# Four matrix products of a decoder layer: weight fetch, input split and norm moved into one stage each

## The chip, the cores and the metric

The kernel runs on one core of a Trainium2 chip. The metric is the device time of one execution in microseconds (us); the kernel before took 5367.47 us (median of 3 runs, 5363.57 to 5371.20).

## The reference, cut to what matters

One inference step of one decoder layer, for 1024 prompt tokens and 64 sample tokens (1088 together), width 1024:

```
h = h + [GatedDeltaNet | Mamba2-SSD](rmsnorm(h) @ w_in) @ w_out     # w_out is 2048 x 1024
h = h + attention(rmsnorm(h, g_xattn) @ w_xq, memory) @ w_xo        # both 1024 x 1024
f = rmsnorm(h, g_ffn)
h = h + peer(f, f @ w_pq)                                           # w_pq is 1024 x 2048
y = rmsnorm(h, g_final)

rmsnorm(x, w) = x * rsqrt(mean(x*x) + 1e-6) * w
```

The change touches the products with w_out, w_xq, w_xo and w_pq and the two norms ahead of w_xq and w_pq. The delta net, the state space scan (SSD), the attention, the top-16 retrieval and the experts are as they were.

## The kernel before, in words

Activations lie transposed: a [128, 8, 1088] tile has the width in 8 slices of 128 partitions (k = 0 to 7) and the tokens along the free dimension, in three chunks of 384, 384 and 320 columns. The residual `h` stays in SBUF from the first of the four products on.

Every product is done in split precision. A 32-bit operand x becomes hi = round(x) in the 32-bit type that TensorE multiplies in one pass, and lo = x - hi; `split_product` (lines 123 to 128) then issues three matmuls, hi*hi, lo*hi and hi*lo, into one PSUM bank. The hi half is an ACT copy; the lo half is a subtraction on DVE or POOL.

`linear` (from line 1557) makes a product. It goes through the outputs in blocks of 128, two to a turn of a hardware loop; r = 0, 1 says which. For a block: SP fetches 512 KB of weights (line 1584), ACT rounds them to `w_hi` (1610), POOL subtracts for `w_lo` (1623), TensorE does 3 chunks x 8 slices x 3 matmuls = 72 matmuls (1633), chunk outermost, slice k inside, and DVE adds the three banks to the residual (1654) or copies them to a stage that SP stores (1650, 1589). Each of these has two buffers, so the weights of a block are made ready while an earlier block is multiplied. The two r's use PSUM banks 0 to 2 and 3 to 5.

`split_tiles` (line 1665) is a stage of its own ahead of three of the products: SP loads (1674), ACT copies each slice to hi (1681), DVE takes the lo of the even slices (1687) and POOL that of the odd ones (1693). Ahead of the other two products stands `rmsnorm` (line 131): ACT squares the 8 slices (164), DVE adds them up (212), TensorE sums over the partitions with 9 matmuls against ones (181; the trace counts 18 instructions), DVE, ACT and DVE make 1/root (214, 167, 216), TensorE spreads it over the partitions (185), DVE multiplies (221, 24 instructions), and the result is split as above (172, 194). Every stage is a `Block` inside a `Phase`: it begins when all engines have ended the one before, and its own weight fetch can begin only then.

The order in `trunk` (from line 2616) is: SSD; `split_tiles` heads_dn; `linear` w_heads_dn (first half of w_out); `split_tiles` heads_ssm; `linear` w_heads_ssm; `rmsnorm` att_norm; `linear` w_xq; attention; `split_tiles` attended; `linear` w_xo; `rmsnorm` ffn_norm; `linear` w_pq; the rest. The SP queue is in program order: a transfer behind a waiting one is not issued.

## Time and profile before

| what | us |
|---|---|
| median of 3 runs | 5367.47 |
| the profiled execution, its own time | 5374.69 |
| its span, first to last instruction | 5372.9 |
| TensorE busy in the span | 4552.5 (85%) |
| w_heads_dn product, first matmul to last | 1762.1 to 1860 |
| w_heads_ssm | 1885.5 to 1983.2 |
| w_xq | 2034.6 to 2131 |
| w_xo | 2321.0 to 2417.8 |
| w_pq | 2469.5 to 2662 |

The times in the lower rows count from the first instruction of the span. Between the products lie the stages that split and normalize; between w_xq and w_xo also the attention, and ahead of w_heads_dn the end of the SSD.

### The profile page before, as it was taken

Reading aid. Unit: us, or ns where it says so; the run is one execution under the profiler, and the core shown is the slowest. Engines: PE = TensorE matmul, PEld = TensorE weight load, DVE = VectorE, ACT = ScalarE, POOL = GpSimd, SP = SyncE. Lnnn points to the kernel's source line nnn. Section 1 sums busy time; section 2 is a strip of 40 time slices with the busy share of each in tenths; the row PEclk is TensorE's granted clock in tenths of the full one; section 3 lists DMA queues with packets and bytes.
Section 4 is the critical chain, followed back from the end, with each engine's and each line's share of the span. In section 5 each row is a group of like instructions: output and inputs, shape, how many; then the busy total and the mean of one; then the engine's idle time right before and its main releaser. Section 6 shows DMA issues by size and latency. Waiting matters only on the chain. (4 is left out here: it accounts for less than half of the span.)

```text
span 5372.9 us, 72522 instructions
## 1 busy us (share of the span) xinstructions
PE 4552.5 (85%) x26809; PEld 4074.5 (76%) x26809; DVE 3182.0 (59%) x6516; ACT 1485.7 (28%) x2869; POOL 1715.0 (32%) x985
## 2 busy tenths in 40 slices
PE   6999999978785777776835666999999999999996
PEld 4677777765553777576834656999999999999996
DVE  2454455534555121212199995777787887778786
ACT  2233333312222111112003552333333333333332
POOL 0111111111111212022102444555555555555552
PEclk9999999989897888988967888999999999999998
DMA  4111111112212202402212437878888887787885
GB/s 149 50 38 44 48 42 37 38 38 59 67 50 84 96 29 85 154 32 99 76 33 79 124 93 252 294 284 291 291 300 291 289 291 282 285 295 288 284 301 189
DMA packets 339412, 825.70 MB, mean 154 GB/s; under 512 B 44334, under 2 KB 227038, under 8 KB 284766
## 3 DMA queue, kind: packets, MB, share of 16 engines
q1 hardware_dynamic: 247006, 373.65, 20.9%
q0 software_dynamic: 55296, 402.68, 20.7%
q10 hardware_dynamic: 36864, 46.15, 2.7%
q8 instruction: 147, 2.41, 0.2%
q14 instruction: 99, 0.81, 0.0%
HBM read 730.19 MB, written 92.21 MB: 153 GB/s over the span
## 5 line engine op out<-in xcount | busy, mean ns | idle before, releaser
L126 PE MATMUL psum_banks<-f_dense_hi,exp_u_hi 128*128 128x352 f32 x2048 | 665.4, 325 | 72.1 <-POOL exp_u_lo L2358 54.4
L2564 DVE CUSTOM_DVE_ANT_0 residual<-residual,f_rows 128x1024 f32<-128x1024 f32 x384 | 672.4, 1751 | 43.1 <-DMA residual<-in_peer_rows,pick_index 42.6
L2367 POOL DMA_INDIRECT residual<-in_peer_rows,pick_index x384 | 516.1, 1344 | 564.1 <-DVE psum_banks L2576 500.1
L126 PE MATMUL psum_banks<-exp_hidden_hi,exp_v_hi 128*128 128x352 f32 x2048 | 660.9, 323 | 8.6 <-issue 7.2
L127 PE MATMUL psum_banks<-f_dense_lo,exp_u_hi 128*128 128x352 f32 x2048 | 661.8, 323 | 0.0
L128 PE MATMUL psum_banks<-f_dense_hi,exp_u_lo 128*128 128x352 f32 x2048 | 661.7, 323 | 0.0
L127 PE MATMUL psum_banks<-exp_hidden_lo,exp_v_hi 128*128 128x352 f32 x2048 | 659.6, 322 | 0.0
L128 PE MATMUL psum_banks<-exp_hidden_hi,exp_v_lo 128*128 128x352 f32 x2048 | 659.4, 322 | 0.0
L663 PE MATMUL psum_banks<-x_normed,dn_weights 128*128 128x384 f32 (+1 forms) x1536 | 526.6, 486 | 20.7 <-DMA dn_conv_w<-in_dn_conv_w 20.7
L2576 DVE SCALAR_TENSOR_TENSOR psum_banks<-residual,exp_coefs,psum_banks 128x1024 f32<-128x1024 f32 x381 | 487.4, 1279 | 0.0
L126 PEld LDWEIGHTS psum_banks<-f_dense_hi,exp_u_hi 128*128 128x128 f32 x2048 | 387.2, 189 | 82.0 <-POOL exp_u_lo L2358 31.6
L953 POOL TENSOR_TENSOR dn_block<-dn_lower,dn_level_masks 128x1152 f32<-128x1152 f32 x56 | 147.2, 2635 | 835.4 <-DVE dn_lower L1027 787.9
L663 PEld LDWEIGHTS psum_banks<-x_normed,dn_weights 128*128 128x128 f32 x1536 | 286.6, 198 | 161.4 <-DMA dn_conv_w<-in_dn_conv_w 21.5
L126 PEld LDWEIGHTS psum_banks<-exp_hidden_hi,exp_v_hi 128*128 128x128 f32 x2048 | 385.3, 188 | 11.3 <-issue 7.4
L2358 POOL TENSOR_TENSOR exp_v_lo<-exp_stage,exp_v_hi 128x1024 fp32r<-128x1024 f32 x128 | 312.5, 2442 | 244.4 <-ACT exp_v_hi L2465 243.4
L128 PEld LDWEIGHTS psum_banks<-f_dense_hi,exp_u_lo 128*128 128x128 f32 x2048 | 387.2, 189 | 0.0
L127 PEld LDWEIGHTS psum_banks<-f_dense_lo,exp_u_hi 128*128 128x128 f32 x2048 | 387.2, 189 | 0.0
L127 PEld LDWEIGHTS psum_banks<-exp_hidden_lo,exp_v_hi 128*128 128x128 f32 x2048 | 385.4, 188 | 0.0
L128 PEld LDWEIGHTS psum_banks<-exp_hidden_hi,exp_v_lo 128*128 128x128 f32 x2048 | 385.4, 188 | 0.0
L2483 ACT ACTIVATE exp_dot_gelus<-exp_dots 128x1 f32<-128x1 f32 x384 | 77.9, 203 | 1020.6 <-DVE exp_dots L2564 1020.4
L2358 POOL TENSOR_TENSOR exp_u_lo<-exp_stage,exp_u_hi 128x1024 fp32r<-128x1024 f32 x128 | 314.1, 2460 | 94.0 <-ACT exp_u_hi L2465 92.8
L2130 POOL TENSOR_TENSOR route_onehots<-route_onehots,route_picked_gates_t 128x512 f32<-128x512 f32 x176 | 183.3, 1041 | 437.9 <-DVE route_onehots L2228 423.7
(465 smaller groups left out, 8643.3 us busy)
## 6 DMA issues: line engine op xcount, KB each, us to landing
exp_stage<-in_peer_u SPq DMA_DIRECT2D x128, 512.0 KB, 4.6
exp_stage<-in_peer_v SPq DMA_DIRECT2D x128, 512.0 KB, 4.0
exp_gates<-expert_gates ACTq DMA_DIRECT2D x256, 176.0 KB, 4.2
expert_gates<-route_gates SPq DMA_DIRECT2D x5, 8192.0 KB, 31.3
dn_weights<-in_w_dn SPq DMA_DIRECT2D x8, 2048.0 KB, 7.3
ssd_row_decay<-gate_rows SPq DMA_DIRECT2D x16, 576.0 KB, 13.4
retrieval_q<-w_pq_stage SPq DMA_DIRECT2D x16, 576.0 KB, 2.8
residual<-retrieval_q SPq DMA_DIRECT2D x9, 1024.0 KB, 6.0
```

The lines of the kernel that those rows point to most:

```text
L126: nc.tensor.matmul(out, w[0], x[0], start=start, stop=False)
L127: nc.tensor.matmul(out, w[0], x[1], start=False, stop=False)
L128: return nc.tensor.matmul(out, w[1], x[0], start=False, stop=stop)
L663: mm = nc.tensor.matmul(PROJECTED[j][c][:, 0:n], w[:, k, j, :], xn[:, k, a:a + n], start=(k == 0), stop=(k == KT - 1))
L953: nc.gpsimd.tensor_tensor(BT[:, l % 2, :].rearrange("p (c n) -> p c n", n=CK), LT[:, :].rearrange("p (c n) -> p c n", n=CK), const["level" ...
L2130: nc.gpsimd.tensor_tensor(E[w % RING][:, 1, :, :], E[w % RING][:, 1, :, :], gateT[:, at][:, :, None].to_broadcast([P, PICK, NK]), ALU.mult ...
L2358: nc.gpsimd.tensor_tensor(lo, stage[:, n % 2, :], hi.bitcast(F32), ALU.subtract).then_inc(lo_done.sem, 1)
L2367: nc.gpsimd.indirect_dma_start(slot[:, n % SLOTS, :, :].rearrange("p x n -> p (x n)"), None, d["peer_rows"], bass.IndirectOffsetOnAxis(ap= ...
L2483: nc.scalar.activation(gelus[:, r:r + 1], dots[:, r:r + 1], ACT.Gelu).then_inc(dot_gelu.sem, 1)
L2564: nc.vector.tensor_tensor_reduce(u, u, xg[:, g, :], 1.0, 0.0, ALU.mult, ALU.add, dots[:, r:r + 1]).then_inc(dotted.sem, 1)
L2576: op = nc.vector.scalar_tensor_tensor(acc, rows, coefs[:, r:r + 1], acc, ALU.mult, ALU.add)
```

## The change

`linear` takes the inputs' split and the norm into its own stage, and `split_tiles` goes.

- Both halves of w_out become one `linear` with two sources (S = 2): the second source's slices are loaded, rounded and subtracted into the same hi and lo buffers while the last block of the first is multiplied. `x_free` counts the slices that this block has done with.
- SP issues in this order: the first `first_w` input slices, the two weight blocks of turn 0, the other slices, the weights of turn 1 (`fetch(1)`, which waits for the split of turn 0), then the `prefetch` list (for w_heads the 8 slices of the residual), then the second source.
- TensorE's loops are turned: slice k outermost, the three chunks inside. In the first block of a source it waits slice by slice for lo.
- The lo halves are dealt out otherwise: DVE takes slices 0, 2, 3, 5, 6 (w_heads, w_xo) or 0, 3, 6 (w_xq, w_pq), POOL the others, between its two weight blocks of turn 0.
- The squares for the next norm are made in the linear ahead of it (`summed`): when a block of the residual is final, ACT squares it and DVE adds it to `acc`; at the end TensorE sums `acc` and the last square into bank 6. `norm` then begins with the mean.
- First and last turn of each source stand outside the hardware loop (`all_turns`).

```diff
-def linear(nc, bank, name, rhs, w, K, outs, tokens, how, to, prefetch=(), behind=None):
+def linear(nc, bank, name, parts, w, outs, how, to, sources, first_w, const, low_on_vector, prefetch=(), behind=None, summed=False, norm=None):
...
+        def all_turns(engine, body):
+            for s in range(S):
+                body(s, 0, True, False)
+                with engine.Fori(1, turns - 1) as i:
+                    body(s, i, False, False)
+                body(s, turns - 1, False, True)
...
             @block.sync
...
+                lead = sources[0][1] is not None
+                if lead:
+                    load(0, range(first_w))
                 fetch(0)
+                if lead:
+                    load(0, range(first_w, KT))
+                fetch(1)
                 for dst, src, sig in prefetch:
                     sp.dma_start(dst, src).then_inc(sig.sem, 16)
+                for s in range(1, S):
+                    load(s, range(KT))
...
             @block.scalar
...
+                def high(s, ks):
+                    for k in ks:
+                        if norm is not None:
+                            act.wait_ge(val_ready.sem, val_ready.at(k + 1))
+                        elif sources[s][2] is not None:
+                            act.wait_ge(sources[s][2][k].sem, sources[s][2][k].at(1))
+                        if s and k < KT - 1:
+                            act.wait_ge(x_free[s - 1].sem, x_free[s - 1].at(k + 1))
+                        elif s:
+                            act.wait_ge(product[1].sem, product[1].at(1, s * turns - 1))
+                        for a, n in spans:
+                            op = nc.scalar.activation(hi[:, k, a:a + n], raw(s)[:, k, a:a + n], ACT.Copy)
+                        op.then_inc(x_hi[s].sem, 1)
+
+                def square(i, r):
+                    act.wait_ge(taken[r].sem, taken[r].at(1, i + (S - 1) * turns))
+                    act.wait_ge(sums.accumulated[r].sem, sums.accumulated[r].at(1, i - 1 + r))
+                    nc.scalar.activation(sums.sq[r][:, 0:T], tile(to, i * 2 + r), ACT.Square).then_inc(sums.squared[r].sem, 1)
+
+                def turn(s, i, first, last):
+                    g = i + s * turns
+                    if first:
+                        if norm is not None:
+                            act.wait_ge(mean_ready.sem, 1)
+                            nc.scalar.activation(rstd[:, :], rstd[:, :], ACT.Sqrt).then_inc(root_ready.sem, 1)
+                        n = 0 if s else first_w
+                        high(s, range(n))
+                        weight(g, 0)
+                        high(s, range(n, KT))
+                        weight(g, 1)
...
             @block.gpsimd
...
+                def turn(s, i, first, last):
+                    g = i + s * turns
+                    weight(g, 0)
+                    if first:
+                        for k in range(KT):
+                            if k not in low_on_vector:
...
+                    weight(g, 1)
...
             @block.tensor
...
-                        for c, (a, n) in enumerate(cols):
-                            for k in range(K):
+                        for k in range(KT):
+                            if first and r == 0:
+                                sig, n = low_ready(s, k)
+                                pe.wait_ge(sig.sem, n)
+                            for c, (a, n) in enumerate(CHUNKS):
                                 mm = split_product(nc, bank[3 * r + c][:, 0:n], (wh[r][:, k, :], wl[r][:, k, :]),
...
+                            if last and r == 1 and s < S - 1 and k < KT - 1:
+                                mm.then_inc(x_free[s].sem, 1)
                         mm.then_inc(product[r].sem, 1)
+                all_turns(pe, turn)
+                if sums is not None:
+                    pe.wait_ge(sums.blank.sem, 1)
+                    pe.wait_ge(sums.accumulated[0].sem, sums.accumulated[0].at(1, turns - 1))
+                    for t in range(NC):
+                        nc.tensor.matmul(SUMMED[:, t:t + 1], sums.acc[:, P * t:P * t + P], ones[:, 0:1], start=(t == 0), stop=False)
+                    pe.wait_ge(sums.squared[1].sem, sums.squared[1].at(1, turns - 1))
+                    for t in range(NC):
+                        nc.tensor.matmul(SUMMED[:, t:t + 1], sums.sq[1][:, P * t:P * t + P], ones[:, 0:1], start=False, stop=(t == NC - 1))
...
             @block.vector
...
+                def values():
...
+                    for k in range(KT):
+                        for c, (a, n) in enumerate(CHUNKS):
+                            op = nc.vector.scalar_tensor_tensor(val[:, k, a:a + n], sources[0][0][:, k, a:a + n], norm[:, k:k + 1],
+                                                                SPREAD[c][:, 0:n], ALU.mult, ALU.mult)
+                        op.then_inc(val_ready.sem, 1)
+                        if k - 1 in low_on_vector:
+                            low(0, k - 1)
...
+                def turn(s, i, first, last):
+                    if first and s == 0:
...
                         if behind is not None:
                             v.wait_ge(*behind)
...
+                    for r in range(2):
+                        if last and r == 1 and s < S - 1:
+                            lows(s + 1)
+                        if sums is not None and s == S - 1:
+                            add_squares(i, r)
+                        v.wait_ge(product[r].sem, product[r].at(1, g))
...
+            linear(nc, bank, "w_heads", parts, d["w_heads"], KT, "add", h, [(heads, loads[x], loaded[x]) for x in range(2)], 2, const,
+                   (0, 2, 3, 5, 6), prefetch=[(h[:, k, :], d["xT"][k], h_loaded) for k in range(KT)],
+                   behind=(h_loaded.sem, h_loaded.at(KT)), summed=True)
...
+                linear(nc, bank, "w_xq", cn, d["w_xq"], KT, "store", qx, [(h, None, None)], 0, const, (0, 3, 6),
+                       norm=const["gains"][:, 1, :],
...
+            linear(nc, bank, "w_xo", parts, d["w_xo"], KT, "add", h, [(ao, None, None)], 4, const, (0, 2, 3, 5, 6), summed=True)
...
+                linear(nc, bank, "w_pq", fn, d["w_pq"], 2 * PHEADS, "store", qp, [(h, None, None)], 0, const, (0, 3, 6),
+                       norm=const["gains"][:, 3, :],
```

## Rows read from the trace of the kernel before

**Rows 1.** The page's first line.

```profile
span 5372.9 us, 72522 instructions
```

**Rows 2.** The waits of TensorE, 1720 to 2700: total, times, longest, in us.

```profile
PE psum_banks L126 <- POOL w_heads_dn_w_lo L1623: 53.9, 1, 53.9
...
PE psum_banks L126 <- POOL w_xo_w_lo L1623: 25.4, 1, 25.4
```

**Rows 3.** Windows in and after first products: length, busy by engine, PEclk, DMA, GB/s.

```profile
1762.10:1777.00 14.90, 14.90 (x74) 14.90 (x75) 0.00 (x0) 0.06 (x1) 2.18 (x1) 0.80 0.65 262
1777.00:1860.00 83.00, 82.93 (x504) 82.66 (x502) 9.91 (x21) 6.31 (x6) 14.32 (x6) 1.00 0.07 25
2321.00:2324.30 3.30, 3.30 (x10) 3.30 (x11) 0.00 (x0) 0.00 (x0) 2.13 (x1) 0.50 0.51 163
```

**Rows 4.** Timeline from the SSD's end to w_heads_dn's first product: start, length (us).

```profile
1732.28 4.50 SPq L1674 DMA_DIRECT2D heads<-mixed_heads  x8
1736.82 5.96 SPq L1674 DMA_DIRECT2D residual<-in_xT  x8
...
1735.77 1.11 ACT L1681 ACTIVATE heads_hi<-heads 128x1088 fp32r<-128x1088 f32 x1 [24.93 <-DMA heads<-mixed_heads]
...
1746.28 1.11 ACT L1681 ACTIVATE heads_hi<-heads 128x1088 fp32r<-128x1088 f32 x1 [0.24 <-DMA heads<-mixed_heads]
1758.48 2.26 ACT L1610 ACTIVATE w_heads_dn_w_hi<-w_heads_dn_w 128x1024 fp32r<-128x1024 f32 x2 [11.09 <-DMA w_heads_dn_w<-in_w_heads_dn]
...
1777.07 1.42 DVE L1654 TENSOR_TENSOR residual<-residual,psum_banks 128x384 f32 x3 [27.89 <-PE psum_banks L128]
```

**Rows 5.** Timeline of DVE from w_heads_dn's last product to w_heads_ssm's first.

```profile
1860.16 1.42 DVE L1654 TENSOR_TENSOR residual<-residual,psum_banks 128x384 f32 x3 [10.51 <-PE psum_banks L128]
...
1900.22 1.42 DVE L1654 TENSOR_TENSOR residual<-residual,psum_banks 128x384 f32 x3 [24.96 <-PE psum_banks L128]
```

**Rows 6.** The tile heads_lo: ns of one, min/median/max; first and last start.

```profile
L1687 DVE TENSOR_TENSOR heads_lo<-heads,heads_hi x8: 1292/2567/3579, 1736.9 to 1871.7; 128x1088 fp32r<-128x1088 f32 x8
L1693 POOL TENSOR_TENSOR heads_lo<-heads,heads_hi x8: 2482/3394/3542, 1738.4 to 1874.1; 128x1088 fp32r<-128x1088 f32 x8
```

**Rows 7.** Timeline from w_heads_ssm's last product to w_xq's first, by engine.

```profile
1983.24 1.41 DVE L1654 TENSOR_TENSOR residual<-residual,psum_banks 128x384 f32 x3 [10.45 <-PE psum_banks L128]
...
1985.91 8.11 ACT L164 ACTIVATE att_norm_squares<-residual 128x1088 f32<-128x1088 f32 x8 [25.40 <-PEq L66]
...
1997.78 4.00 PE L181 MATMUL psum_banks<-const_ones,att_norm_squares 128*128 128x1 f32 x18 [14.71 <-DVE att_norm_squares L212]
...
2001.82 0.17 DVE L214 TENSOR_SCALAR att_norm_rstd<-psum_banks 128x9 f32<-128x9 f32 x1 [4.09 <-PE psum_banks L181]
...
2006.78 12.16 DVE L221 SCALAR_TENSOR_TENSOR att_norm_squares<-residual,const_gains,psum_banks 128x384 f32<-128x384 f32 x24 [4.30 <-PE psum_banks L185]
...
2032.13 4.67 POOL L1623 TENSOR_TENSOR w_xq_w_lo<-w_xq_w,w_xq_w_hi 128x1024 fp32r<-128x1024 f32 x2 [2.47 <-ACT w_xq_w_hi L1610]
...
2048.27 1.42 DVE L1650 COPY w_xq_stage<-psum_banks 128x384 f32<-128x384 f32 x3 [21.60 <-PE psum_banks L128]
```

**Rows 8.** Timeline around the split of the attended heads, ahead of w_xo.

```profile
2297.85 8.11 ACT L1681 ACTIVATE attended_hi<-attended 128x1088 fp32r<-128x1088 f32 x8 [15.39 <-PEq L66]
...
2334.80 1.42 DVE L1654 TENSOR_TENSOR residual<-residual,psum_banks 128x384 f32 x3 [24.04 <-PE psum_banks L128]
```

**Rows 9.** Timeline from w_xo's last product to w_pq's first.

```profile
2417.82 1.42 DVE L1654 TENSOR_TENSOR residual<-residual,psum_banks 128x384 f32 x3 [10.44 <-PE psum_banks L128]
...
2429.27 1.28 ACT L167 ACT_TABLE_LOAD   x1
...
2484.10 1.42 DVE L1650 COPY w_pq_stage<-psum_banks 128x384 f32<-128x384 f32 x3 [22.66 <-PE psum_banks L128]
```

**Rows 10.** Timeline of TensorE in w_xq, where one chunk's bank follows another's.

```profile
2056.14 0.33 PE L128 MATMUL psum_banks<-c_normed_hi,w_xq_w_lo 128*128 128x384 f32 x1
2056.31 0.31 PE L126 MATMUL psum_banks<-c_normed_hi,w_xq_w_hi 128*128 128x320 f32 x1
```

More of the change, by code:

```diff
@@ L1600, in _ @@
                 else:
-                    with sp.Fori(1, turns) as i:
+                    with sp.Fori(2, S * turns) as i:
                         fetch(i)
@@ new lines, in square @@
+                def square(i, r):
[5 more added lines that the diff above has]
+                    if first:
+                        if norm is not None:
+                            act.wait_ge(mean_ready.sem, 1)
[5 more added lines that the diff above has]
+                        weight(g, 1)
+                    else:
+                        for r in range(2):
+                            weight(g, r)
+                            if sums is not None and s == S - 1:
+                                square(i - 1, r)
+                    if last and sums is not None and s == S - 1:
+                        for r in range(2):
+                            square(i, r)
@@ L1612, in _ @@
+                all_turns(act, turn)
             @block.gpsimd
@@ L1619, in _ @@
                         nc.gpsimd.memset(stage[r][:, :], 0.0).then_inc(zeroed.sem, 1)
-                with pool.Fori(0, turns) as i:
-                    for r in range(2):
-                        pool.wait_ge(hi_done[r].sem, hi_done[r].at(1, i))
-                        nc.gpsimd.tensor_tensor(wl[r][:, :, :], wb[r][:, :, :], wh[r][:, :, :].bitcast(F32), ALU.subtract).then_inc(split[r].sem, 1)
+                if sums is not None:
+                    nc.gpsimd.memset(sums.sq[0][:, T:TP], 0.0).then_inc(sums.blank.sem, 1)
+                    nc.gpsimd.memset(sums.sq[1][:, :], 0.0).then_inc(sums.squared[1].sem, 1)
+                    nc.gpsimd.memset(sums.acc[:, :], 0.0).then_inc(sums.accumulated[0].sem, 1)
@@ L1637, in _, with low @@
             @block.vector
             def _(v):
-                if how == "store":
-                    v.wait_ge(zeroed.sem, zeroed.at(2))
-                with v.Fori(0, turns) as i:
-                    for r in range(2):
+                def low(s, k):
+                    v.wait_ge(x_hi[s].sem, x_hi[s].at(k + 1))
+                    for a, n in spans:
+                        op = nc.vector.tensor_tensor(lo[:, k, a:a + n], raw(s)[:, k, a:a + n],
+                                                     hi[:, k, a:a + n].bitcast(F32), ALU.subtract)
+                    op.then_inc(x_lo[s][0].sem, 1)
@@ L1643, in _, with turn @@
+                def turn(s, i, first, last):
+                    g = i + s * turns
+                    if first and s == 0:
+                        if norm is not None:
+                            values()
+                        else:
+                            lows(0)
                         if behind is not None:
                             v.wait_ge(*behind)
-                        v.wait_ge(product[r].sem, product[r].at(1, i))
                         if how == "store":
-                            v.wait_ge(stored[r].sem, stored[r].at(1, i - 1))
@@ L1648, in _ @@
-                        for c, (a, n) in enumerate(cols):
+                            v.wait_ge(zeroed.sem, zeroed.at(2))
+                    for r in range(2):
+                        if last and r == 1 and s < S - 1:
+                            lows(s + 1)
+                        if sums is not None and s == S - 1:
+                            add_squares(i, r)
+                        v.wait_ge(product[r].sem, product[r].at(1, g))
+                        if how == "store":
+                            v.wait_ge(stored[r].sem, stored[r].at(1, g - 1))
+                        for c, (a, n) in enumerate(CHUNKS):
```

154 lines of the change are left out of this document (91 added, 63 removed).

## The prediction, made before the changed kernel had run

> **What bounds the kernel now.** I read the waits of TensorE first, because TensorE is the busiest engine. In the stretch of the four products its long waits are those of the first matmul of each of the five `linear` stages for the weights' lo half: five waits, the longest 53.9 us (it takes in the end of the SSD), the shortest 25.4 [rows 2]. So in these seams TensorE is idle and the end of the kernel moves with them. Inside a product nothing is to be won: after the first block, seven blocks fill 83.0 us at granted clock 1.00, 11.86 us a block, with TensorE busy 82.93 [rows 3]. The timelines of ACT, DVE, POOL and SP then show what each seam is made of. What matters is when the first block of a product ends; DVE's first add or copy starts 0.1 us after it, and I take that start as the mark.
>
> **Clock at a restart.** The first ten matmuls after a gap take 3.30 us at a granted clock of 0.50, which is 1.2 GHz; the whole first block takes 14.9 us instead of 11.86 [rows 3]. I count 14.0 us for a first block that starts cold with its operands there.
>
> **Seam 0, SSD to w_heads.** Count from the first SP load, 1732.28; before, the first block ends 44.8 us later (1777.07) [rows 4]. Now: slice 0 lands at 3.5, and slices follow every 1.5 us (ACT's copies from 1735.77 to 1746.28 are 7 steps) [rows 4]. The order is slices 0 and 1, two weight blocks, slices 2 to 7: 3.5, 5.0, 6.5, 8.0, then 9.5 to 17.0. ACT rounds the first weights 6.5 to 7.6 (2.26 us for two [rows 4]), POOL subtracts in 2.34 (4.67 for two [rows 7]), TensorE starts at 10.1. Slice 7 is rounded at 18.1 and lo, on POOL, at 20.7 (2.5 alone [rows 6]); its nine matmuls end by 22.3. So the first block ends at 24.1, set by TensorE, and the gain is 20.7. Against it stands a new wait. SP now blocks in `fetch(1)` until the second weight block is split, and POOL reaches that only after its three slices: ACT 18.1 to 19.2, POOL 20.7 to 23.1. Behind it in the queue are the eight residual slices; issued from 23.1 they land by 23.1 + 3.5 + 8 x 1.5 = 38.6. DVE can add no block before that (`behind`), so bank 0 is free at 40.1, and TensorE, done with its second block at 24.1 + 11.9 = 36.0, waits 4.1. Bounds 0 (the residual lands in time) to 5 and some 1 in the first block; I take 4. Net **16.7** (14.5 to 20.7). The second source's slices are issued behind the residual and land some 12 us later, long before 24.1 + 7 x 11.9.
>
> **Seam 1, between the halves of w_out.** Before: 1860.16 to 1900.22 is 40.06 us for one block of 11.86, so 28.2 are lost [rows 5, 3]. Now slice k of hi is free when TensorE is through it in the last block, every 1.5 us; ACT copies in 1.1, DVE or POOL subtracts in 1.3 to 3.6 [rows 6]. The chain is faster than the 1.5 x 3 us between POOL's slices; only slice 7 is left when the block ends, is ready about 4 us after, and is wanted 10 us after. Weight copies and bank 0 are ready too. Gain **28.2**; if slice 7 were late, down to 26.
>
> **Seam 2, w_heads to w_xq.** Before, 1983.24 to 2048.27 is 65.0 us [rows 7]. Count from 1983.24. Removed are 8.11 us of squares and the adds behind them, and the fetch that began only after the norm. In their place: the last add 1.4, its square 1.1, at 2.8; the nine sums of `acc` run meanwhile, the nine of the last square follow. One set takes 4.00 at the low clock; the two end at 4.8 to 8.0, I take 6.5. The step to the next stage costs 1.25 (1984.65 to 1985.91), so the new stage begins at B = 7.8. From the mean to the first product with the gain is 4.96 (2001.82 to 2006.78) and stays: B + 5.2. DVE makes a slice in 12.16/8 = 1.52 and does lo 0, 3, 6 between; TensorE starts at B + 9.6 to 10.8 after slices 0, 1 and lo 0. Its pace is then POOL's: value 7 at B + 20 to 22.4 (eight values, lo 0 and lo 3), rounded at B + 21.3 to 23.7; lo 7 on POOL 2.5 to 3.5, later still where POOL is behind; then the second weight block, 2.34. The second block of the product starts at B + 26.2 with uncontended durations and B + 29.7 with the contended ones [rows 6]; I take 28. So the first block ends in effect at 35.8 and the gain is **29.2** (26 to 32.8). All squares but the last, 1.1 on ACT and 1.3 on DVE each, lie beside blocks of 11.86 in which DVE has work for 1.4 and ACT for 1.1 [rows 5, 3], so they cost nothing.
>
> **Seam 3, attention to w_xo.** Before, 2297.85 to 2334.80 is 36.9 [rows 8]. Now four slices are rounded (4.1), then the weights, landed at 3.5 (5.2), split by POOL (7.7), and TensorE starts; lo 1, 4, 7 on POOL are done at 15 to 18, ahead of it. First block done at 21.7. Gain **15.2** (14.3 to 15.2).
>
> **Seam 4, w_xo to w_pq.** Before, 2417.82 to 2484.10 is 66.3 [rows 9]. As seam 2, but ACT's table load of 1.28 now stands at the stage's start, ahead of the root, where before it lay beside the adds, and a slice's hi and lo are two instructions each. Second block at B + 28 to 31.5, I take 29.8; gain **28.7** (25.5 to 32.2).
>
> **Sum.** 16.7 + 28.2 + 29.2 + 15.2 + 28.7 = 118.0 us. The profiled execution took 5374.69 (span 5372.9 [rows 1]), so 5256.7; the median of the runs is 7.2 lower, so **5249.5**. The bounds together give gains of 107 to 129, so 5238 to 5261 for this case. What comes after w_pq is unchanged and moves as a whole.
>
> **The turned loops.** Now 24 groups of three matmuls in a block change the bank each time, before three. Where the bank changes today the next matmul starts 0.17 us after the last, as inside a chunk [rows 10]. I cost it at nothing.
>
> **Rivals.**
> *DVE and POOL block one another fully.* Both subtract from SBUF while the norm's slices are made. Alone they take 1.29 and 2.48 us, side by side up to 3.58 and 3.54 [rows 6]. If a subtraction on DVE waits out a whole one of POOL, 1.3 + 2.5 = 3.8, three of these stand ahead of value 7 or beside it, and POOL's five grow as well: the second blocks start some 4 us later in seams 2 and 4, the time is 5258. For it: the maxima; against it: the medians, and that the products with the gain read PSUM.
> By the Trainium skill, "SBUF — State Buffer", section "SBUF: two separate sides", DVE with two SBUF inputs and GpSimd hold a shared port exclusively. By that rule this rival is the likelier; the trace's 3.58 agrees nearly, its median of 2.57 does not.
>
> *The clock stays low in the stop-and-go blocks.* TensorE's first blocks now begin early and wait slice by slice. If the granted clock stays at 0.50 for a whole first block, its 72 matmuls take 22 us instead of 14. Seams 0 and 3 lose 8 each (seam 0 gets 4 back, as the residual's wait goes), 2 and 4 about 4 each, since there POOL sets the pace: 20 in all, 5270. For it: the restart's rows. Against: in 0 and 3 the operands come faster than TensorE takes them.
> The Trainium skill, "TensorE: Matmul & The Clock Gate", section "HAM oscillation — how this bites in real kernels", says that a wait between every group of matmuls keeps putting the clock back; it speaks for this rival, and the gap rows agree as to whole gaps; no row before shows waits as short as these.
>
> *The seam between the halves does not close.* If the second source's slices came through only after the last block (a late load, or `x_free` seen late), seam 1 would keep what seam 3 keeps, some 13 us: 5263. Against it: 80 us of slack for the loads.
>
> *Slower: changing banks costs.* A matmul's record is 0.33 long, twice the spacing. If a matmul into another bank had to wait for the end of the last, 0.16 us more, then 21 added changes x 48 blocks = 1008 cost 161 us, the time is 5411. It decides from 118/1008 = 0.117 us a change. Against it: [rows 10].
>
> **Numbers.** The forecast 0.62, the full block 0.15, the low clock 0.12, the open seam 0.08, the banks 0.03. For 8 in 10 the range goes from 5234, 4 below the forecast's best sum for the scatter of the runs, to 5278, above the low clock. About 0.2% (11 us) is what a measurement of this kernel can tell from no change; all cases but the last lie far below it: faster 0.96, within 0.01, slower 0.03.
>
> **What would show it.** Between w_heads' eighth and ninth block DVE's adds stand 11.9 apart, like any others. In the third block's place TensorE waits some 4 us for DVE, and DVE for the residual's load. w_xq's first matmul starts some 18 us after w_heads' last, and its second block's wait is put down to POOL's weight split. The step between the loops costs nothing if a steady block still takes 11.86. The prediction is wrong if blocks take longer than that, if the sums at a linear's end take over 8 us, or if a first block lasts over 20 us in seams 0 and 3.

## The result, and the profile after

| kernel | median of runs (lowest to highest), us | ratio to before, 95% interval |
|---|---|---|
| before | 5369.34 (5363.57 to 5379.04) | |
| after | 5291.64 (5284.06 to 5298.45) | 0.9853 (0.9831 to 0.9875) |
| after, timed again later | 5287.71 (5275.35 to 5294.88) | 0.9835 (0.9819 to 0.9851) |

The change is faster by 78 to 89 us, not by the 118 forecast, and the time lies above the range. The page of the profiled execution (5298.45 us) begins [rows 1]:

```profile
span 5296.5 us, 72287 instructions
```

TensorE's waits in the products (waited for: total, times, longest, us) answer to [rows 2]. Of five waits of 25 to 54 us one long one is left, at the SSD's end. A new one of 4.5, DVE's add, is the one that the prediction put into seam 0.

```profile
PE psum_banks L126 <- POOL w_heads_w_lo L1728: 34.7, 1, 34.7
...
PE psum_banks L126 <- POOL w_xo_w_lo L1728: 9.9, 1, 9.9
...
PE psum_banks L126 <- DVE f_dense_lo L1783: 4.6, 1, 4.6
PE psum_banks L126 <- DVE residual L1839: 4.5, 1, 4.5
PE psum_banks L126 <- DVE c_normed_lo L1783: 4.5, 1, 4.5
```

Seam 0 [rows 4], timelines of SP and then DVE (start, length). The first two weight blocks go out at 1730.83; the next two begin at 1740.52, and the second of them waits for the split of the block whose buffer it takes, so that the queue goes on 14.49 us later, and only then with the residual. DVE adds two blocks at once at 1770.81, when the residual is there.

```profile
1729.96 0.82 SPq L1642 DMA_DIRECT2D heads<-mixed_heads  x2
1730.83 0.90 SPq L1629 DMA_DIRECT2D w_heads_w<-in_w_heads  x2
...
1740.52 14.49 SPq L1629 DMA_DIRECT2D w_heads_w<-in_w_heads  x2
1755.05 5.38 SPq L1651 DMA_DIRECT2D residual<-in_xT  x8
```

```profile
1770.81 2.74 DVE L1839 TENSOR_TENSOR residual<-residual,psum_banks 128x384 f32<-128x384 f32 x6 [18.39 <-DMA residual<-in_xT]
1786.23 1.42 DVE L1839 TENSOR_TENSOR residual<-residual,psum_banks 128x384 f32 x3 [12.69 <-PE psum_banks L128]
1798.23 1.42 DVE L1839 TENSOR_TENSOR residual<-residual,psum_banks 128x384 f32 x3 [10.58 <-PE psum_banks L128]
```

Seam 1 [rows 5], DVE: the first block of the second source is added at 1858.11, 59.9 us and five blocks after 1798.23. There is no seam any more.

```profile
1858.11 1.42 DVE L1839 TENSOR_TENSOR residual<-residual,psum_banks 128x384 f32<-128x384 f32 x3 [6.17 <-PE psum_banks L128]
```

Seam 2 [rows 7], TensorE and DVE: the sums of the accumulated squares begin while the last block is added, the last square's follow, and the norm's slices and the split run into the product.

```profile
1941.91 2.06 PE L1773 MATMUL psum_banks<-const_ones,w_heads_acc 128*128 128x1 f32 x18
1944.72 2.38 PE L1776 MATMUL psum_banks<-const_ones,w_heads_squares 128*128 128x1 f32 x18 [0.75 <-ACT w_heads_squares L1690]
...
1957.88 0.66 PE L126 MATMUL psum_banks<-c_normed_hi,w_xq_w_hi 128*128 128x384 f32 x1 [4.49 <-DVE c_normed_lo L1783]
```

```profile
1942.11 1.42 DVE L1839 TENSOR_TENSOR residual<-residual,psum_banks 128x384 f32<-128x384 f32 x3 [8.11 <-PE psum_banks L128]
1948.46 0.17 DVE L1792 TENSOR_SCALAR w_xq_rstd<-psum_banks 128x9 f32<-128x9 f32 x1 [4.94 <-PEq L66]
1953.43 3.11 DVE L1798 SCALAR_TENSOR_TENSOR w_xq_normed<-residual,const_gains,psum_banks 128x384 f32<-128x384 f32 x6 [4.30 <-PE psum_banks L1749]
...
1962.18 1.97 DVE L1783 TENSOR_TENSOR c_normed_lo<-w_xq_normed,c_normed_hi 128x1088 fp32r<-128x1088 f32 x1
...
1974.85 1.42 DVE L1836 COPY w_xq_stage<-psum_banks 128x384 f32<-128x384 f32 x3 [4.29 <-issue]
1987.64 1.42 DVE L1836 COPY w_xq_stage<-psum_banks 128x384 f32<-128x384 f32 x3 [11.37 <-PE psum_banks L128]
```

Seams 3 and 4 [rows 8, 9], DVE:

```profile
2246.51 1.42 DVE L1839 TENSOR_TENSOR residual<-residual,psum_banks 128x384 f32<-128x384 f32 x3 [6.91 <-PE psum_banks L128]
```

```profile
2330.51 1.42 DVE L1839 TENSOR_TENSOR residual<-residual,psum_banks 128x384 f32<-128x384 f32 x3 [8.11 <-PE psum_banks L128]
...
2364.76 1.42 DVE L1836 COPY w_pq_stage<-psum_banks 128x384 f32<-128x384 f32 x3 [4.42 <-issue]
2377.54 1.42 DVE L1836 COPY w_pq_stage<-psum_banks 128x384 f32<-128x384 f32 x3 [11.36 <-PE psum_banks L128]
```

By DVE's marks, against the prediction:

| step | predicted gain, us | measured | from |
|---|---|---|---|
| seam 0 | 16.7 | 12.2 | first SP load to the third block's add: 1777.07 + 23.72 - 1732.28 = 68.5, now 1786.23 - 1729.96 = 56.3 |
| seam 1 | 28.2 | 28.1 | 40.06, now 11.98 |
| seam 2 | 29.2 | 31.2 | to the second block: 76.8, now 45.5 |
| seam 3 | 15.2 | 14.0 | first rounding of the attended heads to w_xo's first add: 2334.80 - 2297.85 = 36.9, now 2246.51 - 2223.55 = 23.0 |
| attention | 0 | 2.8 | last copy of w_xq to that rounding: 166.7, now 163.9 |
| seam 4 | 28.7 | 31.0 | to the second block: 78.0, now 47.0 |
| turned loops | 0 | -5.5 | 39 steady blocks: 11.86, now 12.00 |
| sum | 118.0 | 113.8 | first SP load to w_pq's last mark: 929.6, now 815.6, so 114.0 |

So the products gave what was forecast, within 4 us. That is in part luck: seams 0 and 3 and the turned loops gave 11.2 us less than forecast, seams 2 and 4 and the untouched attention 7.1 more. The loss lies behind them: from w_pq's last copy to the end the kernel before takes 2710 us, the changed one 2750 in this execution and 2732 in that of its second timing. Nearly all of it is in the experts' stage, whose instructions nobody changed: first expert product to last, windows of the two kernels (length, busy of PE, its weight load, DVE, ACT, POOL, clock, DMA share, GB/s):

```profile
3295.30:5322.20 2026.90, 1977.42 (x12288) 1964.95 (x12288) 1596.53 (x2174) 653.11 (x1537) 1138.37 (x637) 0.99 0.81 289
```

```profile
3176.80:5244.70 2067.90, 1992.91 (x12287) 1979.41 (x12288) 1599.58 (x2174) 655.44 (x1537) 1132.00 (x637) 0.99 0.80 283
```

The same 12288 matmuls take 41 us more, and DMA moves 283 in place of 289 GB/s, the same bytes in a longer time. TensorE's waits there, before and after (for exp_u_lo the longest, 31.2 and 30.4, is the stage's start; `issue` is a stop in which it waits for nothing that the profile shows), and the loads' median time to landing:

```profile
PE psum_banks L126 <- POOL exp_u_lo L2358: 54.4, 23, 31.2
PE psum_banks L126 <- DVE exp_hidden_lo L2549: 17.7, 9, 2.2
PE psum_banks L126 <- issue: 7.2, 1, 7.2
```

```profile
PE psum_banks L126 <- POOL exp_u_lo L2511: 69.2, 25, 30.4
PE psum_banks L126 <- issue: 21.8, 4, 9.6
PE psum_banks L126 <- DVE exp_hidden_lo L2702: 13.7, 7, 3.0
```

```profile
exp_stage<-in_peer_u SPq DMA_DIRECT2D x128, 512.0 KB, 4.6
residual<-in_peer_rows,pick_index POOLq DMA_INDIRECT x384, 7.3
```

```profile
exp_stage<-in_peer_u SPq DMA_DIRECT2D x128, 512.0 KB, 5.1
residual<-in_peer_rows,pick_index POOLq DMA_INDIRECT x384, 8.0
```

A turn of this stage (32 of them, 63.0 us in the mean before, 64.2 after) has 61.1 us of matmuls. The turn's last u weight, the first of the next turn, is issued 13.8 us after the turn's start, and TensorE wants its lo half at 23.0. In between stand its landing (5.6 us in the mean before, 6.2 after), ACT's 1.05 and POOL's 2.4: 22.9 us before, so hardly any slack, and 23.5 after. In 15 of 31 turns, in both kernels, ACT was also still busy with a GELU when the load had landed, so the load is not the only thing that makes this weight late.

By TensorE's gaps beyond the regular spacing of 0.159 us, 82 us were lost in the stage before and 123 after: 32 and 54 at this weight, 25 and 36 at a turn's first product, 9 and 12 ahead of the last turn's output products. The second profiled execution of the same changed program (e9) lost 105: 39 at this weight, 38 at a turn's first product. So the weight carries 22 of 41 us in one execution and 7 of 24 in the other, and one profile is not enough to say where the loss sits.

At a turn's first product the traces show another kind of loss. Of the `issue` rows the longest is the one ahead of the last turn's output products. The three others after, 3.7 to 4.4 us, stand where TensorE's loop returns to its start; e9 has two (3.5 and 4.7), the kernel before none. In each a 16 KB code fetch lands, and TensorE goes on 1.6 to 1.7 us after the landing, so I take them for waits for its own code. After such a stop it runs at the low clock for a while; here are the 5 us that follow the one of 4.4 us, with the granted clock (0.55) behind the engines:

```profile
4341.60:4346.60 5.00, 4.97 (x18) 4.98 (x19) 0.00 (x0) 0.00 (x0) 1.42 (x2) 0.55 0.72 241
```

The granted clock stood at 0.50 for 17 us of the stage before and for 55 us after, and TensorE is busy 15.5 us longer with the same matmuls (1992.91 for 1977.42).

### The profile page after: what moved, and what is told of

Its sections match the earlier page's. It is cut to its first block and busy times, and to the rows that moved or that the text cites. A ratio compares the mean times of both kernels' runs of the same rounds, so it can differ in the third digit from the quotient of the medians.

```text
span 5296.5 us, 72287 instructions
## 1 busy us (share of the span) xinstructions
PE 4575.1 (86%) x26845; PEld 4095.5 (77%) x26845; DVE 3195.8 (60%) x6518; ACT 1489.4 (28%) x2861; POOL 1712.9 (32%) x987
## 5 line engine op out<-in xcount | busy, mean ns | idle before, releaser
L126 PEld LDWEIGHTS psum_banks<-exp_hidden_hi,exp_v_hi 128*128 128x128 f32 x2048 | 385.3, 188 | 13.8 <-issue 9.8
```

The costliest lines, as they stand in the source:

```text
L126: nc.tensor.matmul(out, w[0], x[0], start=start, stop=False)
```

## The experiments

In the table, rest is the time from w_pq's last copy to the end in the profiled execution (2710 before, 2750 after). Each run was timed beside the kernel before on the same chip.

| run | median, us | ratio, 95% interval | rest |
|---|---|---|---|
| e1 | 5277.51 | 0.9821 (0.9806 to 0.9835) | 2745 |
| e2 | 5386.75 | 1.0023 (1.0013 to 1.0034) | 2737 |
| e3 | 5375.47 | 1.0007 (0.9997 to 1.0017) | 2721 |
| e4 | 5282.75 | 0.9833 (0.9820 to 0.9847) | 2736 |
| e5 | 5280.00 | 0.9832 (0.9815 to 0.9849) | 2729 |
| e6 | 5282.52 | 0.9833 (0.9820 to 0.9846) | 2733 |
| e7 | 5390.74 | 1.0031 (1.0019 to 1.0043) | 2735 |
| e8 | 5282.31 | 0.9837 (0.9824 to 0.9850) | 2727 |
| e9 (after, again) | 5287.71 | 0.9835 (0.9819 to 0.9851) | 2732 |
| e10 | 5274.18 | 0.9816 (0.9803 to 0.9830) | 2724 |
| e11 | 5270.74 | 0.9807 (0.9794 to 0.9821) | 2727 |
| e12 | 5288.16 | 0.9834 (0.9821 to 0.9848) | 2739 |
| e13 | 5392.36 | 1.0028 (1.0015 to 1.0041) | 2730 |
| e14 | 5278.40 | 0.9812 (0.9791 to 0.9834) | 2724 |
| e15 | 5260.66 | 0.9790 (0.9770 to 0.9810) | 2719 |
| e16 | 5399.55 | 1.0047 (1.0031 to 1.0062) | 2741 |
| e17 | 5256.83 | 0.9780 (0.9765 to 0.9796) | 2704 |
| e18 | 5265.56 | 0.9794 (0.9774 to 0.9814) | 2735 |

**Where TensorE's code lies (e1, e2).** Code fetches of 16 KB show in the trace as a queue of their own; the loop of three turns takes eleven of them each time round.

```diff
# e1, ahead of the experts' loop on TensorE (e2: 25 and 2, in the kernel before)
+for _ in range(38):
+    nc.tensor.matmul(bank[0][:, 0:1], const["ident"][:, :], const["ones"][:, 0:1], start=True, stop=True)
+for _ in range(5):
+    pe.wait_ge(lo_done.sem, 1)
```

> The changed kernel with 38 one-column matmuls and 5 waits that are already met, put on TensorE where it waits some 31 us for the first expert rows anyway. They only move the code behind them, so that the experts' loops stand against the 16 KB instruction fetches as in the kernel before (they stood 6464 bytes off). Theory 'code position' (the 41.4 us that the experts' stage got longer, 2085.2 to 2126.6 us, come from where TensorE's loop code lies): experts' stage back to 2085 to 2095 us, time about 5255 us, ratio to before about 0.979. Rival 'landing' (the gathered rows and weights land later because the transfers fall otherwise in time): stage stays near 2126, time about 5292, ratio 0.9855. Rival 'chance of the execution': the stage lies somewhere between and differs between executions of one kernel.

> The kernel before with 25 one-column matmuls and 2 met waits at the same place, so that the experts' loops on TensorE stand against the 16 KB fetches as in the changed kernel. Theory 'code position': experts' stage 2120 to 2130 us in place of 2085.2, time about 5408 us, ratio 1.0075. Rivals 'landing' and 'chance': stage about 2085, time about 5369, ratio 1.000.

Half of it each time: 14 us off (10 by the second timing of the changed kernel), 15 us on. But e2's loop does not lie as the changed kernel's does: it takes twelve code fetches a round and 123 in the stage, the changed kernel's eleven and 114. After seven of its nine returns TensorE stops 12 products later, 10.5 us in all, and goes on 1.2 to 1.6 us after a code fetch has landed; the changed kernel never stops there. So e2 shows that a place of the code can cost 15 us, much of it by TensorE's own stops. It does not show what the changed kernel's place costs. e2's stops in the stage, with one of 3.7 at a return and the last turn's 6.7:

```profile
PE psum_banks L126 <- issue: 20.9, 9, 6.7
```

The rows of the gathers were the other suspect. A code fetch began during 134 of the 382 gathers after the first two in the kernel before, 170 in the changed one and 169 in e2; such gathers landed in 7.32, 8.17 and 7.53 us, the others in 7.23, 7.45 and 7.29. The Trainium skill, "DMA: Bandwidth & Descriptors", section "Queues, rings and completion order", has each DMA engine take turns between its queues, a packet at a time; that fits, though no record here names the engine. But a longer gather is also likelier to have a fetch begin in it. And late gathers did not reach TensorE by way of DVE, whose exp_hidden_lo it waited for 17.7 us before and 13.7 after. e1's padding was not hidden, as its timeline of TensorE shows; the expert weights were ready at 3177.9:

```profile
3170.21 16.34 PE L2589 MATMUL psum_banks<-const_ones,const_ident 128*128 128x1 f32 x76 [22.75 <-PEq L66]
3186.41 0.64 PE L126 MATMUL psum_banks<-f_dense_hi,exp_u_hi 128*128 128x352 f32 x1
```

**Input placement, the other engines' code (e3, e5, e6, e7).**

```diff
# e3, in the kernel before: one input of 8 MB
-d["w_heads_dn"] ... d["w_heads_ssm"]
+d["w_heads"][0:KT] ... d["w_heads"][KT:2 * KT]
# e5, after: e1 and, ahead of the experts' code, met waits on DVE, POOL and SP
+for _ in range(232):    # 126 on POOL, 110 on SP
+    v.wait_ge(al_ready.sem, 3)
# e6: e1 with two inputs of 4 MB. e7: e3 with all engines' code shifted
```

> The kernel before with the two halves of w_out in one input of 8 MB, fetched by slices of it, as the changed kernel has them; nothing else differs. Theory 'input placement' (the experts' tables lie elsewhere in memory or are bound otherwise, so that gathers land later: 7.78 in place of 7.28 us in the mean): experts' stage about 2125 us, time about 5405 us. Theory 'code position' and the rival 'landing': no change, 5369 us, ratio 1.000.

> The changed kernel with the code of TensorE, DVE, POOL and SP before the experts' loops lengthened by one-column matmuls and waits already met, so that each of these engines' code from there on stands against its instruction fetches exactly as in the kernel before. So far: aligning TensorE alone gave 14 us back (5277.5 us), shifting it in the kernel before cost 15. Theory 'code position is the whole of it': everything from w_pq's end on takes what it took before, time 5255 to 5260 us, ratio 0.979. Rival 'only TensorE's code matters, the rest is where the one 8 MB input puts the tables': no more than TensorE alone gave, 5275 to 5280 us, ratio 0.982.

> The changed kernel with w_out's halves as two inputs of 4 MB, as before, and TensorE's code aligned. Gathers beside which no code fetch fell landed in 7.21 and 7.28 us in the two kernels with two inputs, in 7.43 to 7.62 in the four with one. Theory 'input placement': that difference goes too, 7.2 to 7.3 us, time about 5260 us, ratio 0.979. Rival (the other engines' code, or chance): they land in 7.4 to 7.6 and the time is that of TensorE aligned alone, 5277 us, ratio 0.982.

> The kernel before with one 8 MB input for w_out and the code of TensorE, DVE, POOL and SP shifted to where it stands in the changed kernel: both suspects at once, nothing of the change itself. If they are the whole of the loss, the rest behind w_pq gets some 34 us longer: 5405 us, ratio 1.0063. If they only add up as measured alone (15.5 and 4.2 us), 5391 us, ratio 1.0037; what is missing then comes from elsewhere.

Neither suspect holds for the whole: e3 differs by less than can be told from none (its interval reaches 9 us), e5 and e6 gave no more than e1 (the padding of e1, e5 and e6 makes the first expert product 9 to 11 us late). e7 costs what e2 and e3 cost together, and has e2's twelve fetches a round.

**The two small terms of the products (e4, e8).**

```diff
# e4
-                fetch(1)
                 for dst, src, sig in prefetch:
                     sp.dma_start(dst, src).then_inc(sig.sem, 16)
+                fetch(1)
# e8, in every block but a source's first and w_out's middle one
-for k in range(KT): for c in range(3)
+for c in range(3): for k in range(KT)
```

> The changed kernel with the residual's eight slices issued ahead of the second weight block in w_heads, so that they don't stand behind SP's wait for the split of that block. My reckoning of seam 0: TensorE's wait of 4.5 us for DVE goes, and the clock's restart of some 2 us behind it, so about 6 us less: ratio to the changed kernel about 0.9988, 5285 us where the changed kernel has 5292. Rival: the second weight block lands later, behind the residual's slices, by some 5 us; then TensorE waits for it instead and the gain is under 2 us. If the experts' stage depends on where code lies, this kernel may differ there too, since SP's code moves, and only the marks up to w_pq's end are to be compared.

> The changed kernel with the loop over the three chunks outermost again in every block that isn't a source's first or the last of w_out's first half; so many instructions and the same length of code. Theory (a change of bank costs some 7 ns): a steady block falls from 12.00 to 11.86 us, 42 blocks, 6 us: 5285.5 us, ratio 0.9842 where the changed kernel has 0.9853. Rival (the 0.14 us comes from something else in the block): blocks stay at 12.00, 5291.6 us.

Both expectations held where they can be seen, in the products: from the first SP load to w_pq's end 808.8 us in e4, 6.8 less than after, and 4.5 less in e8, where 6 were expected. In e4 the residual is issued at once, and DVE adds the first block 27.4 us after the first SP load, not 40.9:

```profile
1733.47 7.01 SPq L1652 DMA_DIRECT2D residual<-in_xT  x8
1740.53 12.46 SPq L1629 DMA_DIRECT2D w_heads_w<-in_w_heads  x2
```

```profile
1755.24 1.42 DVE L1842 TENSOR_TENSOR residual<-residual,psum_banks 128x384 f32<-128x384 f32 x3 [4.86 <-DMA residual<-in_xT]
```

In the whole time neither gain can be told from the repeated after (e9).

**Position again, hidden, and another one (e9, e10, e11, e12).**

```diff
# e10, e11: at the end of the route stage; e12: 6 in place of 38
+for _ in range(38):
+    nc.tensor.matmul(bank[4][:, 3 * P:3 * P + 1], const["ident"][:, :], const["ones"][:, 0:1], start=True, stop=True)
+for _ in range(4):
+    pe.wait_ge(once.sem, once.at(3))
# e11, e12: with the edits of e4 and e8
```

> The changed kernel unaltered, timed on the same chip as the next three so that they have a base: 5292 us, ratio 0.9853 if the first timing holds; 5285 if its four runs lay high.

> As e1_after_pe_aligned, TensorE's loop code of the experts where it lay in the kernel before, but with the padding at the end of the route stage, where TensorE has 30 us of nothing to do; at its first place it was not hidden: its matmuls ran from 3170.2 to 3186.5 us and the first expert product, whose operands were ready at 3177.9, began 8.5 us late. Theory 'code position': another 8 us, 5269 us, ratio 0.981, so that position alone accounts for some 22 of the 37 us that the rest lost. Rival (the pad's delay was made up later by the loads being ahead): 5277 us as in e1.

> Three edits together: chunks outermost in the steady blocks (4.6 us by the products' trace), the residual ahead of the second weight block (6.7 us) and the hidden padding of e10. If they add up: 10 to 12 us below e10, 5258 us, ratio 0.979.

> The same as e11 with 27 instructions of padding in place of 155, which puts the experts' loop 8192 bytes away from where it lay before (1088 in place of 9280, counted in 16 KB). Theory 'code position': a time of its own, as far from e11 as e1 was from the changed kernel (10 to 25 us), either way. Rival (position matters little, differences are chance): within 5 us of e11.

Position is worth 13.5 us in e10, less than expected, and the intervals of e9 and e10 overlap; it is worth 17 between e11 and e12, which differ in the length of the padding alone; there 37 and 54 us are lost at the late u weight. In the products e11 gained 7.8 us over e10, not 11, and 3.4 of them show in the medians.

The runs together say more than a pair. What the products gained, less what the whole kernel gained by its median, is the loss behind them. Where the loop lies elsewhere it is 36 and 25 us (after, twice), 32 (e4), 27 (e8) and 33 (e12). Where hidden padding puts it back it is 12 (e10), 16 (e11), 16 (e14) and 5 (e15). With padding that is not hidden it is 20 to 23 (e1, e5, e6). The groups do not overlap: 31 us in the mean against 14 for e10 and e11, or 12 with e14 and e15, whose program is shorter too. So position is worth some 17 us. In the first group a code fetch begins during 20 to 23 of the 31 loads of the late u weight, in the others during one or none. The load lands in 5.9 to 6.2 us in the first, 5.5 to 5.8 in the others, 5.6 before. But in e2 and e7 a fetch falls into 22 of these loads too, and they land no later than the rest, so a fetch beside the load is not enough.

**Length of the program (e13, e14, e15).**

```diff
# e13, TensorE in the kernel before, three of its linears
-with pe.Fori(0, turns) as i: turn(i)
+for i in range(turns): turn(i)
# e14, TensorE after: the first turn inside the loop
-if first and r == 0:
+if r == 0:
-all_turns(pe, turn)
+for s in range(S):
+    with pe.Fori(0, turns if s == S - 1 else turns - 1) as i: turn(s, i, True, False)
+    if s < S - 1: turn(s, turns - 1, False, True)
# both with hidden padding; e15: e14 with the edit of e4
```

> The kernel before with TensorE's loops of three linears (both halves of w_out and w_xq) written out, four turns each instead of a loop: the same work in the same order, but 180224 bytes more of code, about what the change adds (186688), and eleven more fetches of 16 KB before the experts. Hidden padding puts the experts' loop exactly where it lay in the kernel before. Theory 'length of the program' (a longer program moves where things lie or how the fetches fall, and the experts' stage loses some 15 us by it whatever its own position): 5386 us, ratio 1.003. Rival (length costs nothing by itself): 5371 us, ratio 1.000.

> The changed kernel with TensorE's first turn of each product kept in its loop (the waits for the slices stand in every turn, where they are met from the second on), and only the last turn of w_out's first half written out: TensorE's code is 32768 bytes longer than before in place of 186688. Hidden padding puts the experts' loop where it lay before. Theory 'length of the program': with position and length both back, the rest behind w_pq takes what it took before, 5258 us, ratio 0.979. Rival: as with position alone (e10), 5274 us, ratio 0.9816.

> As e14, and the residual's slices ahead of the second weight block: 6.7 us less in seam 0 by the trace of e4. 5251 us, ratio 0.978, if that gain reaches the end; the same as e14 if the experts' stage takes it back.

e13 says yes: nothing but 176 KB more code ahead of an unmoved loop, and 15 us more (0.15 to 0.41%). e14 says no: the short program did not get them back, and took 5278.40 us where e10 took 5274.18. e15 is 17.7 us below e14, of which 7.0 show in the products. So whether length counts in the changed kernel stays open. In e14 the u weight is no longer late: its load lands in 5.8 us, and 34 us are lost there, for 32 before. What is left stands at a turn's first product, 35 us for 25, with two stops of 3.6 and 4.0 us at the loop's return. Four layouts of the kernel before (e2, e3, e7, e13) were 4 to 17 us slower than it, and no layout of the changed one came back to a rest of 2710; e15 came nearest, with 2719.

**The load on the path (e16, e17, e18).**

```diff
-ORDER = [("v", 0, 0), ("v", 1, 0), ("u", 3, 0), ("v", 2, 0), ("u", 0, 1), ("v", 3, 0), ...
+ORDER = [("v", 0, 0), ("v", 1, 0), ("u", 3, 0), ("u", 0, 1), ("v", 2, 0), ("v", 3, 0), ...
# POOL: low u3, gather, low u0 of the next turn, gather, low v2, low v3
# ACT rounds v2 and v3 at steps 4 and 5 of a turn, not 2 and 4
```

> The kernel before with one exchange in the experts' stage: the first u weight of the next turn is fetched, rounded and split ahead of the third v weight instead of behind it (its stage buffer then comes free some 4 us earlier), with two gathers of rows moved one place up on POOL. In the traces TensorE reaches that u weight 23.0 us after a turn's start and its lo half ends at 23.7 before the change, 24.2 after it, because its load, issued at 13.7, lands in 5.7 and 6.2 us. Theory 'one load on the path' (what code position and program length change is when this load lands, and TensorE waits for it in most of the 32 turns): the wait goes, the excess at that place falls from 40 us to under 10, time about 5340 us, ratio 0.994. Rival (the rows' gathers and DVE set the turn): the turns stay at 62.4 us, 5371 us.

> The changed kernel with the same exchange and nothing else; position and length as they are in it. Theory 'one load on the path': the wait goes here too (64 us of excess to under 10), and with it most of what layout costs: the difference to e16 is then the 114 us that the products gained, 5226 us, ratio 0.973, and not the 82 us that the change brought in all. Rival (layout acts through the gathers and DVE as well): the difference to e16 stays at some 82 us, 5258 us.

> The changed kernel with everything that helped: the exchange of e17, TensorE's loops compact with the experts' code where it lay before, the residual ahead of the second weight block, chunks outermost in every second block. If the gains add up: 5226 less 7 for the residual and 2 for the order, 5217 us, ratio 0.971; layout should then no longer count.

The place of the wait is confirmed: in all three the loss at that weight falls from 32 and 54 us to 1.3. What was to follow from it is not: e16 is slower than before, e17 gains 31 to 35 us, and between them lie 143 us, neither 114 nor 82. e18, where all gains were to add up to 5217 us, took 5265.56, though its products are 7.2 us shorter than e17's. The waits of TensorE in e16 and in e17 tell why:

```profile
PE psum_banks L126 <- POOL exp_u_lo L2358: 33.3, 2, 32.2
PE psum_banks L126 <- DVE residual_dense L2558: 29.1, 19, 2.1
PE psum_banks L126 <- POOL exp_v_lo L2358: 22.8, 19, 4.4
```

```profile
PE psum_banks L126 <- POOL exp_u_lo L2511: 32.9, 2, 30.5
...
PE psum_banks L126 <- DVE residual_dense L2711: 16.2, 15, 2.4
PE psum_banks L126 <- POOL exp_v_lo L2511: 11.1, 10, 4.4
```

The exchange made the v weights late in place of the u weight (the third's lo half ends 6 us later in the turn, the fourth's 2.4), and DVE's adds with them. How late differs again between layouts: 70 us are lost in the output products of e16, 37 in e17 and 63 in e18, 9 in the kernel before. So the three runs show that this wait can be taken away, not that it was what the change cost. e17 is the lowest time of all, with the narrowest spread (5255.3 to 5259.8); e15 lies within its interval.

## Why the prediction was wrong

The step that failed is the last sentence of **Sum**: "What comes after w_pq is unchanged and moves as a whole." Its instructions are unchanged, its time is not: 22 to 40 us longer by the profiled executions, 25 to 36 by the medians (114 less 89 and 78). Shown is that the time is lost in the experts' stage, and that the place of TensorE's code is the larger part of it: some 17 us between the two groups of layouts, and 17 between e11 and e12, which differ in nothing else. Shown too is that length alone can cost 15 us in the kernel before (e13).

How the place acts is argued, not shown by a run. The traces put most of it at the late u weight: 39 to 54 us are lost there in the first group, 33 to 39 in the second. TensorE's stops at the loop's return, 12 and 8 us, come in both groups of layouts. That the place acts through the gathers is not shown; TensorE's waits for DVE did not grow. Open are the 5 to 16 us that stay lost with the code back in its place (e10, e11, e14, e15). Input placement and the other engines' code did not give them back (e5, e6).

The other steps, by their own names:

- **Seam 0** was mis-sized by 4.5 us. The wait came as told, 4.5 us for 4.1. But the residual, behind the second block's split, was issued 25.1 us after the first load for the 23.1 reckoned, since POOL's last slice and its weight split, beside DVE's, took 3.64 and 3.43 us for the 2.5 and 2.34 that stand in the sum:

```profile
1747.62 3.64 POOL L1738 TENSOR_TENSOR heads_lo<-heads,heads_hi 128x1088 fp32r<-128x1088 f32 x1 [1.11 <-ACT heads_hi L1684]
...
1751.22 3.43 POOL L1728 TENSOR_TENSOR w_heads_w_lo<-w_heads_w,w_heads_w_hi 128x1024 fp32r<-128x1024 f32 x1
```

  And the third block restarted at a lower clock, for which nothing was in the sum: 13.9 us at a granted clock of 0.88, in the window of that block:

```profile
1772.20:1786.10 13.90, 13.82 (x74) 13.82 (x75) 1.35 (x4) 0.00 (x0) 0.00 (x0) 0.88 0.77 307
```

  e4 takes 6.8 us of this away.
- **Seam 1** closed as forecast; DVE's and POOL's slices were ahead all the way.
- **Seams 2 and 4** gave 2 us more each: the accumulated sums ran at full clock (2.06 us, not 4.00) beside the last add, so in seam 2 the next stage began 6.35 us after the last mark, not 7.8. There, from the mean to the values it took 4.97 for 4.96. The first matmul came 9.4 us later for 9.6 to 10.8.
- **Seam 3** gave 1.2 less, just under its bounds: TensorE began 7.9 us after the stage's start for 7.7, and its first block took 14.9 us for 14.0.
- **The turned loops** were costed at nothing and cost 0.14 us a block, 7 ns for each of 21 added bank changes, 5.5 us in all; e8 returns 4.5. That blocks take longer than 11.86 was a sign of being wrong that the prediction had named. The rows shown of one change could not tell 7 ns.
- Of the rivals, the price of full blocking did not come where it was feared, in the norm's slices: a subtraction on DVE took 1.97 us beside POOL's, not 3.8. It began in the middle of one of POOL's, and 1.97 is its own 1.28 and about what that one had left; the Trainium skill's rule of the exclusive port ("SBUF — State Buffer", "SBUF: two separate sides") agrees with these rows of POOL, the second of which is 0.5 longer. In seams 0 and 3 it came near the full price: DVE's longest took 3.63 and 3.59 us, and POOL's 3.64 and 3.58. There TensorE waited only 0.4 us in each for a lo half. The rows of seam 2:

```profile
1960.47 2.52 POOL L1738 TENSOR_TENSOR c_normed_lo<-w_xq_normed,c_normed_hi 128x1088 fp32r<-128x1088 f32 x1 [0.20 <-ACT c_normed_hi L1684]
1963.48 3.07 POOL L1738 TENSOR_TENSOR c_normed_lo<-w_xq_normed,c_normed_hi 128x1088 fp32r<-128x1088 f32 x1 [0.49 <-ACT c_normed_hi L1684]
```

  The low clock did not last a block: the first blocks of seams 0 and 3 took 15.0 and 14.9 us, at granted clocks of 0.85 and 0.82, under the 20 that were to decide. The rival's 22 us for a block at the low clock should have been 23.7 (twice 11.86), and its time some 5273. The seam between the halves closed. A bank change decides from 117 ns; it took 7.

The range failed with the sum: it had room for seams that give less, none for a stage downstream that takes more. The waits of the whole kernel would have shown that stage's state: the row of 54.4 us for exp_u_lo stands in the kernel before, with 22 waits in 31 turns behind the one at the stage's start.

## What to carry to other kernels

That code is unchanged does not make its time a constant. Before a sum lets "the rest" move as a whole, read the rest's waits: a load that the busiest engine waits for in most turns, by a microsecond each, is a stage whose time hangs on how its transfers fall, and 1 to 2% of that stage belong into the range. Where such a stage is to be explained, profile each kernel twice: here two executions of one program put the loss in different places. A run that moves code is to be checked by its code fetches (e2 had twelve a round for eleven). Judge an edit by the marks of its own stage first; 6.8 us were plain there and hardly to be seen in the whole time.

## What the runs showed of the hardware

- Two executions of the same program differ by 18 us in this stage alone (2067.9 and 2050.3 us), so small gains need the stage's own marks.
- 27 instructions of padding in place of 155, far ahead of a loop, changed the whole time by 17 us (e11, e12).
- TensorE can stop where its loop returns: 3.3 to 5.1 us, once to three times in ten rounds of several layouts, and each time it goes on 1.6 to 1.8 us after a 16 KB code fetch has landed (after, e1, e3, e9, e14).
- With two gathers of a turn 3.5 us earlier (e16 to e18), DVE's product over the gathered rows took 1.39 to 1.42 us in the mean in place of 1.71 to 1.81; in e16 the whole time grew all the same.
